# Reordering the head of a fused transformer program: x before the modulations, query units before context units

## The reference, cut to what matters

```python
mod   = silu(c) @ w_mod + b_mod          # 6 x 1024 values: sh1, sc1, g1, sh2, sc2, g2
mod_c = silu(c_ctx) @ w_mod + b_mod      # only csh1, csc1 of it are needed
h  = rms_norm(x)   * norm1_g * (1 + sc1)  + sh1      # 1024 tokens
hc = rms_norm(ctx) * norm1_g * (1 + csc1) + csh1     # 256 context tokens
q_a, k_a, v_a, q_b, k_b, v_b = split(h @ w_in)       # w_in: 1024 x 2304
k_ac, v_ac, k_bc, v_bc       = the same columns of hc @ w_in (its queries aren't used)
q_a, k_a: rms_norm over each head of 64, then axial rope; q_b, k_b: rms_norm over each head
```

## Time and profile before

| | us |
|---|---|
| median of 3 runs | 2549.24 (2549.12 to 2550.74) |
| the profiled execution | 2551.25 |
| span of its trace | 2549.4 |
| TensorE busy | 2470.8 |
| VectorE, GpSimd, ScalarE busy | 1686.3, 1245.6, 1096.0 |
| first product of the projection starts | 57.04 |
| unit 0 and unit 1 done | 80.2, 87.05 |
| attention starts | 321 |

### The profile page before, as it was taken

One profiled execution on the slowest core, in us unless ns is written; L12 is line 12 of the kernel. 1 busy time (PEld: TensorE's weight loads), 2 busy tenths in 40 slices (PEclk: granted clock), 3 DMA queues, 4 the chain that ended last, 5 costly groups with the idle time before them and its releaser, 6 DMA issues.

```text
span 2549.4 us, 32143 instructions
## 1 busy us (share of the span) xinstructions
PE 2470.8 (97%) x11857; PEld 1983.9 (78%) x11857; DVE 1686.3 (66%) x1952; ACT 1096.0 (43%) x1746; POOL 1245.6 (49%) x735
## 2 busy tenths in 40 slices
PE   7999999999999999999999999999999999998997
PEld 5778778888778888887786777777877788887885
DVE  5673278897267656659988311234179988889988
ACT  4652467877353332334334321234244434434344
POOL 0224122583475555556876211124476655556875
PEclk9999999999999999999999999999999999999999
DMA  7462010234212232225223111011412222236221
GB/s 299 133 201 80 23 50 18 71 99 144 83 61 89 87 112 83 75 89 217 86 81 117 33 34 42 25 34 63 144 50 75 83 91 83 70 116 218 88 88 66
DMA packets 78070, 235.89 MB, mean 93 GB/s; under 512 B 8763, under 2 KB 12987, under 8 KB 77788
## 3 DMA queue, kind: packets, MB, share of 16 engines
q1 hardware_dynamic: 77916, 233.84, 27.0%
HBM read 180.59 MB, written 39.85 MB: 86 GB/s over the span
## 4 chain that ended last, share of the span: by engine, by line
PE 79%; DVE 13%; issue 4%; ACT 2%; DMA 1%; POOL 0%; SPq 0%; DVEq 0%; ACTq 0%
PE S L538 12%; PE S L539 12%; PE S L903 9%; PE S L907 9%; PE S L904 9%; PE S L941 3%; PE S L942 3%; PE S L945 3%; PE MM L775 2%; PE S L775 2%; PE S L749 1%; DVE pl L2229 1%; DVE xt L1986 1%; PE MM L763 1%; PE S L750 1%
## 5 line engine op out<-in xcount | busy, mean ns | idle before, releaser
L2552 POOL TENSOR_TENSOR wbl<-rf,wbh 128x512 fp32r<-128x512 f32 x256 | 396.5, 1555 | 248.5 <-ACT wbh L1401 248.3
L2429 POOL TENSOR_TENSOR wl<-raw,wh 128x1024 fp32r<-128x1024 f32 x58 | 146.9, 2534 | 547.6 <-ACT wh L1149 547.6
L2552 POOL TENSOR_TENSOR wbl<-wq,wbh 128x512 fp32r<-128x512 f32 (+1 forms) x168 | 274.5, 1646 | 110.4 <-ACT wbh L1401 110.3
L1401 ACT ACTIVATE wbh<-rf 128x512 fp32r<-128x512 f32 x256 | 158.3, 627 | 296.2 <-PE S L907 215.8
L903 PE MATMUL S<-th_t,wbh 128*128 128x512 f32 x640 | 251.4, 393 | 0.9 <-issue 0.6
L907 PE MATMUL S<-tl_t,wbh 128*128 128x512 f32 x640 | 250.9, 392 | 0.0
L904 PE MATMUL S<-th_t,wbl 128*128 128x512 f32 x640 | 250.3, 391 | 0.0
L538 PE MATMUL S<-hh,wh 128*128 128x512 f32 x448 | 191.1, 427 | 12.5 <-DVE gt L2360 3.9
L941 PE MATMUL S<-ph,wbh 128*128 128x512 f32 x472 | 187.7, 398 | 15.8 <-DVE xt L2133 7.9
L1401 ACT ACTIVATE wbh<-wq 128x512 fp32r<-128x512 f32 (+1 forms) x168 | 99.0, 594 | 217.8 <-PE S L945 115.3
L903 PE MATMUL S<-th_b,wbh 128*128 128x512 f32 x480 | 189.4, 395 | 2.8 <-DVE cu L2030 1.9
(11 more groups left out here) (392 smaller groups left out, 6101.8 us busy)
## 6 DMA issues: line engine op xcount, KB each, us to landing
mr<-in_w_modT SPq DMA_DIRECT2D x32, 512.0 KB, 4.9
wq<-in_w_d SPq DMA_DIRECT2D x64, 256.0 KB, 5.6
xq<-hid SPq DMA_DIRECT2D x16, 1024.0 KB, 5.2
rf<-in_w_f1g SPq DMA_DIRECT2D x22, 512.0 KB, 3.5
rf<-in_w_f1u SPq DMA_DIRECT2D x22, 512.0 KB, 3.2
hid<-pr SPq DMA_DIRECT2D x22, 512.0 KB, 2.6
rf<-in_w_f2g SPq DMA_DIRECT2D x22, 512.0 KB, 3.4
rf<-in_w_f2u SPq DMA_DIRECT2D x22, 512.0 KB, 3.3
```

What stands on the lines that cost most here:

```text
L1401: e.activation(flat(wbh[wslot(f, n)][:, :, :])[:, 0:x.shape[1]], x, ACT.Copy).then_inc(*w_hi.mark((f, n)))
L2429: e.tensor_tensor(l, raw[:, w % 3, 0:n], h.bitcast(F), ALU.subtract).then_inc(*w_lo.mark(w))
L2552: e.tensor_tensor(l, x, h.bitcast(F), ALU.subtract).then_inc(*w_lo.mark((f, n)))
```

## The change

Loads: SP issues first c, c_ctx (as single rows) and the constants, then the eight x tiles, now 512 KB without the context, then slab 0, the modulation slabs one by one in the order of their use (scale 0, shift 0, slab 1, scale 1, shift 1, then scale k and shift k for k = 2 to 7), then the context as one 1 MB transfer `xc`, slab 2 and the rope tables.

Sums of squares: VectorE adds the squares of tiles 0 to 6 into `x2h`; TensorE sums that and tile 7, four matmuls in place of 24. The context gets a sum of its own, during unit 2. c is spread over the partitions by four one-row matmuls into S[1] and S[2], which ScalarE copies out. One activation table set with both Ln and Exp is loaded ahead.

Modulations: a block now has c stationary (two columns) and the weights moving (128 columns), which gives two rows; ScalarE copies them to `mt`, and a small matmul turns them back to a column (`mod_turn`). TensorE makes ten of the sixteen (eight shifts, scales 0 and 1), VectorE the other six scales. Gains and shifts are made for each k, and used in one ScalarE operation with scale and bias.

Order: `UNITS` begins with the four q units of a, then k of a and k of b; the weights are laid out to match. Units 0 and 1 are made together k by k, high products of both, a turn and the next block between, then low products of both. The context is squared, summed, scaled and split during units 0 to 3, and first used by unit 4. Context products take bank `M[u % 2]`. The 32 later modulation rows are spread 2, 4, 4, 5, 5, 6, 6 over units 2 to 8. The twelve bf16 matmuls are gone.

```diff
-NPM = 8
+NPM = 10
-UNITS = [("k", 0, True)] + [("k", m, False) for m in range(4)] + [("q", m, True) for m in range(4)]
+UNITS = [("q", m, True) for m in range(4)] + [("k", 0, True)] + [("k", m, False) for m in range(4)]
-ROPED, VALUES = 8, 13
+ROPED, VALUES = 4, 13
+CONTEXT = 4
+MODS = [("scale", 0), ("shift", 0), ("scale", 1)] + [("shift", _k) for _k in range(1, 8)]
+MOD_ROWS = {2: 2, 3: 4, 4: 4, 5: 5, 6: 5, 7: 6, 8: 6}
...
+        def context_sum(u):
+            return M[u % 2][:, 0:256]
...
+            e.wait_ge(*d_acc(6))
+            for r in HALF:
+                e.matmul(S[j][:, r], ONE, x2h[:, r], start=True, stop=False)
+            e.wait_ge(*a_sq(("ms", 7)))
+            for r in HALF:
+                i = e.matmul(S[j][:, r], ONE, xq[:, 1, r], start=False, stop=True)
+            i.then_inc(*summed.mark("ms"))
...
+            def mod_block(kind, k):
...
+                for x in range(8):
+                    i = e.matmul(M[n % 2][0:2, 0:128], csl[:, 2 * x:2 * x + 2], w[:, 128 * x:128 * x + 128],
+                                 start=x == 0, stop=x == 7)
...
+            for u in range(2):
+                SL.take(e, u, (d_ev, u))
+                e.wait_ge(*w_hi(u))
+                e.wait_ge(*w_lo(u))
             for k in range(8):
+                e.wait_ge(*a_hh(("in", k)))
+                for u in range(2):
+                    step(u, u, 8, 128, k, SL.of[u], hh, hl, parts=(0, 1))
+                if k == 0:
+                    mod_turn("scale", 1)
+                if k < 7:
+                    mod_turn("shift", k + 1)
+                if k < 6:
+                    mod_block("shift", k + 2)
+                e.wait_ge(*d_hl(("in", k)))
+                for u in range(2):
+                    i = step(u, u, 8, 128, k, SL.of[u], hh, hl, parts=(2,))
...
                 if s == 2:
-                    unit_sums(0)
+                    first_sum = SL.take(e, ("sum", 0), (a_ln, 0))
+                    fill[0] = context_sums
+                    fill[1] = lambda: unit_sums(0, first_sum)
```

On ScalarE:

```diff
             for k in range(8):
+                n = MODS.index(("shift", k))
+                e.wait_ge(*turned(("mod", n)))
+                e.activation(pair_of(M_MOD, k, 48), mod_sum("shift", k), ACT.Identity,
+                             bias=vec[:, V_BMOD + k:V_BMOD + k + 1]).then_inc(*a_mod.mark(("shift", k)))
                 e.wait_ge(*d_xr(k))
...
+                e.activation(xw[k][:, :], xw[k][:, :], ACT.Identity, bias=mv[:, M_MOD + k:M_MOD + k + 1],
+                             scale=mv[:, M_G1 + k:M_G1 + k + 1]).then_inc(*a_aff.mark(k))
...
                 unit_norm(s - 1)
                 if s + 2 < NU:
                     split_hi(s + 2)
+                if s in (2, 3):
+                    context_in(s - 2)
```

On VectorE:

```diff
+            scaled(0)
+            gain(0)
+            scaled(1)
+            scale_row(2, 0)
+            low(0)
+            gain(1)
+            for k in range(2, 8):
+                scaled(k)
+                if k > 2:
+                    scale_row(k, 0)
+                scale_row(k, 1)
+                gain(k)
+                low(k - 1)
+            context_squares()
+            low(7)
...
             unit_take(0)
             unit_take(1)
+            context_scaled()
             unit_norm(0)
-            mod_rows(1)
             for s in range(2, NU):
                 if s >= 3:
                     unit_rope(s - 3)
                 if s < NU - 1:
                     unit_norm(s - 1)
+                if s in (2, 3):
+                    context_low(s - 2)
```

On SP:

```diff
+            for k in range(8):
+                e.dma_start(xw[k][:, :], T["xT"][k][:, 0:1024]).then_inc(*l_x.inc(k))
+            load_slab(0)
+            load_block(0)
+            load_block(1)
+            load_slab(1)
+            load_block(2)
+            load_block(3)
+            for k in range(2, 8):
+                load_row(k)
+                load_block(2 + k)
+            e.dma_start(xc[:, :, :], T["xT"][:, :, 1024:1280].rearrange("a p c -> p a c")).then_inc(*l_xc.inc(0))
             load_slab(2)
```

More of the change, by code:

```diff
@@ L540, in step @@
                     if cx is not None:
-                        i = e.matmul(M[jc][0:mm, 0:256], lhs, cx[n // 2][:, k, :], start=first, stop=last)
+                        i = e.matmul(context_sum(name), lhs, cx[n // 2][:, k, :], start=first, stop=last)
                 return i
@@ L561, in gemm @@
                 j = SL.take(e, name, *back)
-                jc = ML.take(e, name, *back_c) if cx is not None else None
+                if cx is not None:
+                    for signal_, event in back_c:
+                        e.wait_ge(*signal_(event))
                 e.wait_ge(*w_hi(w))
@@ L576, in gemm, with gemm_pair @@
                 return j
-            def gemm_pair(names, ws, ready, ready_lo, backs, backs_c=(None, None), cx=None, mms=(128, 128), fill=(), both=4, warm=0):
-                j, jc = [0, 0], [None, None]
+            def gemm_pair(names, ws, ready, ready_lo, backs, mms=(128, 128), fill=(), both=4, warm=0):
+                j = [0, 0]
                 def begin(a):
                     j[a] = SL.take(e, names[a], *backs[a])
-                    if cx is not None:
-                        jc[a] = ML.take(e, names[a], *backs_c[a])
                     if a == 0:
@@ new lines, in mod_turn @@
+            def mod_turn(kind, k):
+                n = MODS.index((kind, k))
+                e.wait_ge(*a_mod(("row", n)))
+                e.wait_ge(*(mod_read(n - 2) if n >= 2 else a_ln("ms")))
+                e.matmul(mod_sum(kind, k), mt[0:2, n % 4, :], ID[0:2, 0:2], start=True, stop=True).then_inc(*turned.mark(("mod", n)))
+            mod_block("scale", 0)
+            mod_block("shift", 0)
+            mod_turn("scale", 0)
+            mod_turn("shift", 0)
+            mod_block("scale", 1)
@@ L657, in unit_sums @@
+            SL.back[0] = [(a_mod, ("shift", 6)), (a_mod, ("shift", 7))]
+            ML.back = [[(a_mod, ("row", 8))], [(a_mod, ("row", 9))]]
             def unit_sums(u, j=None):
@@ new lines, in mod_row @@
+            def mod_row(kind, k):
+                n = MODS.index((kind, k))
+                e.wait_ge(*mod_made(n))
+                if n >= 4:
+                    e.wait_ge(*turned(("mod", n - 4)))
+                e.activation(mt[0:2, n % 4, :], M[n % 2][0:2, 0:128], ACT.Copy).then_inc(*a_mod.mark(("row", n)))
+            split_hi(0)
+            spread(0)
+            e.wait_ge(*summed("ms"))
+            e.activation(rs[:, 0:1024], S[SL.of["ms"]][:, :], ACT.Ln, bias=EPS).then_inc(*a_ln.mark("ms"))
@@ new lines, in context_in @@
+            def context_in(half):
+                for k in range(4 * half, 4 * half + 4):
+                    if k == 0:
+                        e.wait_ge(*d_xr("context"))
+                    e.activation(xc[:, k, :], xc[:, k, :], ACT.Identity, bias=mv[:, M_CMOD + k:M_CMOD + k + 1],
+                                 scale=mv[:, M_GC + k:M_GC + k + 1]).then_inc(*a_aff.mark(("c", k)))
+                    e.wait_ge(*a_aff(("c", k)))
+                    e.activation(hch[:, k, :], xc[:, k, :], ACT.Copy).then_inc(*a_hh.mark(("inc", k)))
@@ L1187, in unit_norm @@
                 if kind == "v":
[L1188 removed]
+                    c = 128 * m
                     e.wait_ge(*turned(u))
```

302 lines of the change are left out of this document (170 added, 132 removed).

## The result

The changed kernel takes **2556.94 us**, the median of 11 runs (2555.12 to 2563.78). The kernel before, in 11 runs on the same chip, took 2551.27 (2549.12 to 2558.04). The ratio is 1.0022, interval 1.0014 to 1.003. So the change makes it **slower by 5.7 us**, where 6.0 us less was forecast. That is 0.22%, just past the 0.2% that can be told from no change, and the time lies outside the range. Of the 13.7 us between 2556.94 and the forecast 2543.2, 11.7 belong to the change; the other 2.0 are the kernel before, whose first three runs had a median of 2549.24.

The account below looks back on a forecast made before the run. TensorE, busy 2470.8 of 2549.4 us, was taken as the bound. Lead 11.8 + removed wait 1.7 + gaps 3.95 - give-backs 11.5 = 6.0 us less, from the median 2549.24 to 2543.2; range 2536 to 2551, 8 times in 10.

Parts of the forecast that it names:

- The head: Start of the kernel: sums of squares end at 24.1, blocks take 1.7 each, first product at 32.5 instead of 57.0.
- The pair: Query units 0 and 1, made k by k: 5.15 us per k, VectorE slowest, last products at 69.05 us.
- The stalls: TensorE's waits for slab 2's split and the squares of units 1, 2, 3: 3.1, 3.8, 2.8 and 1.35 us.
- Together 11.5: Sum of what the new order gives back: the four waits plus 0.45 us for the context's sum, 11.5 us.
- rival A: Cold start: clock 0.50 up to about 40 us, where the products then start; time 2550.7; chance 0.15.
- the 1.7: TensorE's old wait for the square ahead of unit 1's sums, 1.7 us, forecast to go away.
- the gaps: Five TensorE waits of 0.56 us between successive context units; alternating banks remove them, 3.95 us in all.
- B: Slower: blocks pull the clock down inside the pair, 9.2 us per k; three such give 2562.7; chance 0.07.
- C: Lead kept: queues run further ahead, waits for squares are covered, 8 us less given back, time 2535; chance 0.15.
- D: No difference: a later load or queue binds, time 2549.2; chance 0.05.
- Table loads: ScalarE: no drain, by the trace; the skill's 1.38 us drain would lengthen unit 1's square wait by 1.4, time 2544.6.

Follow-up runs that it names:

- silu_later: Changed kernel with, on ScalarE, slab 3's split ahead of unit 0's norm and cb's Silu behind unit 1's norm; 2555.3 us, ratio 1.0017.
- take_first: Changed kernel with VectorE copying units 2 and 3 out of PSUM before making the context's low halves; 2552.67 us, ratio 1.0002.
- earlier_turns_warm: earlier_turns plus eleven bf16 matmuls with unused result right behind the pair, in TensorE's wait for slab 2's low half; 2539.69 us, ratio 0.9961.
- head_warm: both_orders plus 18 short bf16 matmuls on TensorE in the idle time ahead of the sums of squares; 2544.83 us, ratio 0.9972.
- earlier_turns: both_orders with c's second spread and slab 1's split ahead of Ln, turns behind unit 0's high products, unit 0 finished whole at k = 7; 2541.82 us.
- both_orders: Changed kernel with the edits of take_first and silu_later together; 2544.51 us, ratio 0.997.
- thin_blocks: Changed kernel with the six modulation blocks inside the pair making one of their eight matmuls (shifts 2 to 7 incomplete); 2569.97 us, one run.

## Why the prediction was wrong, step by step

**The head, mostly right.** x tile 7's square came at 17.15 (17.4 forecast), and Ln and Exp followed without a table load. The sums took 6.6 where I took 5.6, a value between the slow and the fast price; the row to go by was that of before's first, slow sums. Part of this miss is chance: with the same head, silu_later's profile has the sums in 5.1 us and the first product at 33.49, and take_first's has 34.19. Their end was 26.1 instead of 24.1. The first product came at 35.02 instead of 32.5, **2.5 late**: the 2.0 of the sums, and 0.4 of GpSimd's low half, 2.82 instead of 2.41 beside VectorE. The blocks were right: 1.75 each against 1.7.

**The pair, right by the step, wrong at its end: 3.3 us.** A step took 5.22 (5.15 forecast), but I had called VectorE the slowest by little and ended the pair with its low(7). The ScalarE loop, which I put at 4.8, takes 5.2 as well. The last `hh` came only at 71.7, and behind it stood the high products of both units for k = 7 (1.9) and the last low ones. I had counted only the latter behind VectorE's end. Where three engines run level, the last item of each must be followed to the end.

**The stalls, right in place and cause.** All four are there, in the order forecast: 3.28, 3.89, 4.00 and 2.44 us against 3.1, 3.8, 2.8 and 1.35, 2.6 more in all. The last two are 2.3 us longer because the context's low half took 2.12 us, and I had taken it for a subtraction of 1024 columns like the others, 1.14; and because an affine of 256 columns took 0.59, not 0.49:

```profile
103.97 2.12 DVE L1917 TENSOR_TENSOR hcl<-xc,hch 128x1024 fp32r<-128x1024 f32 x1 [5.88 <-ACT hch L1307]
106.01 1.21 DVE L1936 COPY qa<-S 128x1024 f32<-128x1024 f32 x1
```

What made it slow is GpSimd's rope, which was already under way: 102.61 to 105.00 us, beside the first 1.0 of this operation. The traces of the experiments have other overlaps, and the operation is longer by just as much. With 1.0 us beside the rope it takes 2.12, with 1.1 (earlier_turns_warm) 2.22, with 1.5 (head_warm) 2.61 and with 1.9 (earlier_turns) 2.94. What is left is 1.1 each time, what a subtraction of 1024 columns takes from start to start; its operands, four rows of 256 with gaps between them, cost nothing more.

**The step that failed: "Together 11.5".** There I priced each give-back at the length of its wait, and nothing behind it. The clock fell behind three of the four, and the work that followed ran at 1.2 GHz: 6.1 us against both_orders, which still has two waits of 0.6, and 6.9 by difference (15.3 less 2.5, 3.3 and 2.6). So the new order gave back 21.0 us by unit 4, where the step has 11.5: 2.6 in the waits and 6.9 behind them. Of the 15.3 lost this is the largest term, but not the only one: the other three make 8.4, so with a clock at 1.00 throughout, the gain of 6.0 would still have been gone.

I had weighed idleness as a cause of a cold start for the head (rival A), and did not ask the same of the waits that the change itself makes. The longest wait for a square before was 1.7 us, with 1.00 behind it, and I looked no further than 320 us. Behind that, the trace of before has other waits of this length, and the clock falls at some of them: at 504.7 us (1.80), 617.7 (1.60), 1370.9 (2.44) and 2355.1 (4.75). (Not at the same ones in each profile: in that of the changed kernel it stays at 1.00 from 500 to 520 and from 1360 to 1400 us.)

```profile
2355.08 0.73 PE L941 MATMUL S<-ph,wbh 128*128 128x512 f32 x1 [4.75 <-DVE xt L2133]
```

```profile
1371.00:1377.00 6.00, 6.00 (x16) 3.81 (x17) 6.00 (x7) 1.61 (x3) 2.83 (x2) 0.72 0.00 0
2355.00:2359.00 4.00, 3.92 (x10) 3.14 (x11) 4.00 (x5) 0.00 (x0) 3.93 (x3) 0.57 1.05 402
```

Of full speed, 0.28 of 6 us and 0.43 of 4 us are missing, 1.7 us each. So the price could be read before the run. As an estimate from these two rows, three stalls at 1.7 cost 5.1 us more, which leaves 0.9 of the 6.0: no difference that a measurement tells, in place of a gain. The Trainium skill ("TensorE: Matmul & The Clock Gate", Part 1, the HAM clock gate) has throttled as the default state, which activity releases; I had applied that to the head alone. The traces agree with it at the three stalls (0.50 at 108 and 128 us, behind 4.00 and 2.44 of idleness), but not at every wait: 1.00 stood behind the 3.28.

**Gone as forecast:** the 1.7, and the gaps; the v units now follow at 15.17 us. Behind unit 4 the two kernels have the same waits.

**The rivals.** A named the slow clock but tied it to the head, up to 40 us; there the slow pace was over when the blocks began at 26.1. B said that the blocks would pull the clock down in the pair; it stood at 1.00 there, and fell in the one execution of thin_blocks. C and D did not happen. No rival had the mechanism that decided: a reorder that leaves TensorE's work alone, turns one wait of 1.7 us into three of 2.4 to 4.0, and pays for the clock besides.

**Table loads.** In the changed kernel ScalarE's load at 86.45 lasts 1.28, and the Silu behind it starts at 87.75, with nothing between; the operation ahead of the load ends at 86.44. The Trainium skill ("ScalarE: Activation LUTs", What ACT_TABLE_LOAD costs) adds a drain of about 1.38 us; the trace after does not show one either.

## What to carry to other kernels

Price a wait of the busiest engine as its length plus what the clock does behind it: here most waits of 2.4 to 6 us cost some 1.6 to 3.2 us more each, some cost nothing (3.28 in the changed kernel, 2.44 in silu_later), and behind those of 0.6 the clock stayed at 1.00. Look for such waits in the whole trace, not only where the change is. When work is moved from one engine's queue to another place, ask first what stands directly ahead of the operation that TensorE waits for; two swaps of order were worth 12.4 us here. And before cutting work that is "hidden" on TensorE, look at whether it is what keeps the clock up.

## What the runs showed of the hardware, unexpected

- The granted clock reads 1.00 in every window ahead of 35 us in the changed kernel, and in 16 to 20 us before, though the same half-products take 1.65 and 1.87 us there and 0.86 later. In the first microseconds the slow pace shows in the durations and not in the clock's rows; the traces don't say why.
- Eight one-row matmuls of 512 columns kept TensorE at work for 7.16 us without a gap, at 0.9 each, and what came behind them was slow: the sums in the changed kernel (3.57 us for the first two of four half-products, after 4.6 idle), and in head_warm even the bf16 filling put directly behind them, 6.25 us for 18, where 17 took 3.84 in a wait later on.
- Waits of one length had either clock behind them. The 2.44 us wait has 0.50 behind it in the changed kernel (128 to 130 us) and 1.00 in silu_later. The one of 3.28 us, at 78 us, has 1.00 in the profiles of the changed kernel and both_orders, and 0.57 to 0.79 in others; in silu_later and head_warm the clock was low behind 1.68 us already. It differs from one execution to the next, and so does the time, by some 2 us.
- A subtraction of VectorE that starts while GpSimd's rope is running takes 1.1 us plus the overlap: 2.12, 2.22, 2.61 and 2.94 us for overlaps of 1.0, 1.1, 1.5 and 1.9. That is the time it would take if it stood still until the rope had ended.
- Steps with only 1.37 us of idleness in each 5.2 also ran slowly in one execution, once the blocks between were thinned out.
- A filling whose result is thrown away kept the clock at 1.00 behind each wait that it fitted into, worth 3.7 us for three waits, and 2.1 for one, where the ranges overlap. Where it stood behind another wait, or ran past the wait's end, the median did not move.
